# Sparse-attention stage: order of weight loads and bias rows, compressed bias by TensorE, gate row read from DRAM, gate products with stationary weights

## What is computed

```python
def nsa_mixer(h, rel_bias, w_in, ...):           # 16 heads of 64, 4 key/value groups
    q, kc, vc, ks, vs, kw, vw, gl = jnp.split(h @ w_in, cuts, axis=-1)
    kc = rms_norm(compress_blocks(kc, ...)); vc = compress_blocks(vc, ...)   # 31 compressed keys
    gates = jax.nn.sigmoid(gl).reshape(b, t, G, R, 3)
    dist_c = tq[:, None] - cmp_end[None, :]       # cmp_end = 16 n + 31
    lg = einsum(q, kc) * scale + bias_tbl[:, :, t5_bucket(dist_c)]
    p_c = masked_softmax(lg, dist_c >= 0);  o_c = einsum(p_c, vc)
    # o_s: the same with selected keys ks, vs; o_w: with the window's keys kw, vw; both with
    # bias_tbl[..., t5_bucket(distance)] over all distances
    o = gate[..., 0:1] * o_c + gate[..., 1:2] * o_s + gate[..., 2:3] * o_w
    return o @ w_out
# around it: mod = silu(c) @ ada_w + ada_b; shift, scale, gate = split(mod)
#            x = x + gate * nsa_mixer(rms_norm(x) * (1 + scale) + shift, ...)
```

## Time and profile before

| | us |
|---|---|
| three runs, median (lowest to highest) | 3502.08 (3494.92 to 3509.1) |
| the profiled execution, its own time | 3497.12 |
| its span in the trace | 3495.3 |
| PE busy in the span | 3260.8 (93%) |
| DVE, ACT, POOL busy | 2040.7, 1438.8, 155.5 |

### The profile page before, as it was taken

The page is one execution under the profiler, slowest core; times in us unless marked ns, Lnnn a source line. Parts: engine busy times, 40 slices in busy tenths (PEclk is TensorE's granted clock), DMA queues, the critical chain, the costliest instruction groups (busy, mean ns, idle before and its releaser), DMA issues. The chain is left out here.

```text
span 3495.3 us, 40219 instructions
## 1 busy us (share of the span) xinstructions
PE 3260.8 (93%) x15458; PEld 2605.5 (75%) x15458; DVE 2040.7 (58%) x2660; ACT 1438.8 (41%) x1946; POOL 155.5 (4%) x191
## 2 busy tenths in 40 slices
PE   7999998999999999998999969788999879999995
PEld 6888776788878888757888858545688658877884
DVE  4554426545545553354554445354788768868886
ACT  4222225322232222353222132264588646646884
POOL 0000000000000000000000000242000000001000
PEclk9999999999999999999999989799999989999998
DMA  5332230333223321341332141300799731119995
GB/s 200 127 144 108 101 108 3 151 138 144 108 91 145 144 109 53 139 115 79 138 156 114 60 150 37 73 1 25 299 419 416 286 120 61 61 52 396 417 415 211
DMA packets 96872, 534.19 MB, mean 153 GB/s; under 512 B 18816, under 2 KB 19712, under 8 KB 48336
## 3 DMA queue, kind: packets, MB, share of 16 engines
q1 hardware_dynamic: 85488, 491.24, 36.8%
q0 software_dynamic: 6624, 24.12, 1.8%
q10 hardware_dynamic: 4608, 16.78, 1.2%
HBM read 508.95 MB, written 32.06 MB: 155 GB/s over the span
## 5 line engine op out<-in xcount | busy, mean ns | idle before, releaser
L453 ACT ACTIVATE ffn_silu_gate<-ffn_gate_up 128x512 f32<-128x512 f32 x88 | 52.6, 598 | 960.3 <-PE ffn_gate_up L117 960.3
L515 DVE TENSOR_TENSOR ffn_product<-ffn_silu_gate,ffn_gate_up 128x512 f32<-128x512 f32 x88 | 60.5, 688 | 558.5 <-ACT ffn_silu_gate L453 558.5
L2620 DVE TENSOR_TENSOR moe_low<-moe_raw,moe_high 128x2048 fp32r<-128x2048 f32 x144 | 326.5, 2286 | 30.8 <-ACT moe_high L2537 30.7
L115 PE MATMUL ffn_down<-ffn_down_high,ffn_hid_high 128*128 128x512 f32 x704 | 282.6, 401 | 1.5 <-DVE x_tok L539 1.3
L539 DVE SCALAR_TENSOR_TENSOR x_tok<-ffn_down,x_tok 128x512 f32<-128x512 f32 x352 | 232.8, 687 | 82.6 <-PE ffn_down L117 81.2
L116 PE MATMUL ffn_down<-ffn_down_low,ffn_hid_high 128*128 128x512 f32 x704 | 281.0, 399 | 0.0
L117 PE MATMUL ffn_down<-ffn_down_high,ffn_hid_low 128*128 128x512 f32 x704 | 280.4, 398 | 0.0
L115 PE MATMUL ffn_gate_up<-ffn_h_high,w 128*128 128x512 f32 x704 | 280.2, 398 | 0.0
L116 PE MATMUL ffn_gate_up<-ffn_h_low,w 128*128 128x512 f32 x704 | 278.4, 395 | 0.0
L2537 ACT ACTIVATE moe_high<-moe_raw 128x2048 fp32r<-128x2048 f32 x144 | 274.2, 1917 | 9.9 <-PE moe_bank L117 9.9
L117 PE MATMUL ffn_gate_up<-ffn_h_high,w 128*128 128x512 f32 x704 | 278.2, 395 | 0.0
(11 more groups left out here) (609 smaller groups left out, 7174.0 us busy)
## 6 DMA issues: line engine op xcount, KB each, us to landing
moe_raw<-in_moe_w SPq DMA_DIRECT2D x192, 1024.0 KB, 8.3
ffn_raw_gate_up<-in_ffn_gate_up SPq DMA_DIRECT2D x85, 1024.0 KB, 6.3
ffn_ada_w<-in_ada_w SPq DMA_DIRECT2D x32, 1536.0 KB, 7.1
ffn_raw_down<-in_ffn_down SPq DMA_DIRECT2D x88, 512.0 KB, 3.4
mixer_w_raw<-in_mix_w SPq DMA_DIRECT2D x22, 1024.0 KB, 5.2
hgrn_w_raw<-in_hgrn_w SPq DMA_DIRECT2D x19, 1024.0 KB, 5.2
moe_y<-moe_y ACTq DMA_DIRECT2D x32, 512.0 KB, 9.4
nsa_w_raw<-in_nsa_w SPq DMA_DIRECT2D x13, 1024.0 KB, 5.6
```

The lines of the kernel that those rows point to most:

```text
L115: pe.matmul(out, lhsT[0], rhs[0], start=first, stop=False)
L453: act.activation(silu_gate[slot][:, :], gate_up_ps[2 * slot][:, :], ACT.Silu).then_inc(silu_done, 1)
L515: dve.tensor_tensor(product[slot][:, :], silu_gate[slot][:, :], gate_up_ps[2 * slot + 1][:, :], ALU.mult)\
L2620: dve.tensor_tensor(low[n % SPLITS][:, :, :], raw[n % RAWS][:, :, :], high[n % SPLITS][:, :, :].bitcast(FP32), ALU.subtract)\
```

## The change

Four things. SyncE issues halves 3 and 4 before it waits for the bias rows, and half 5 before `bias_copies`. The compressed bias comes from PE: 31 products whose stationary operand is a slice of 128 distances of a reversed one-hot table (`buckets` is doubled to 1280 columns, its second half reversed) and whose moving operand is `table`, 16 columns, into `cmp_rows` (128 x 31 x 16); VectorE fills `cmp_bias` from that, and its wait for the strip moves to just before the selected attention. The gate row is read from DRAM with one broadcasting DMA issued after the strip; the rows are stored by three DMAs at the end of SyncE's work in the first mixer stage, and `diag` and the GROW products go. The gate products have the 48 gate weights stationary and 512 tokens moving, 24 in place of 96; the result is feature-major, takes its sigmoid so, and four transposes (GATES_T) bring it back.

```diff
 # mixer, block.sync
             weights.fill(sp, 4)
+            if layer == 0:
+                store_modulation(sp, chip, 0)
...
 # nsa, block.sync
             sp.dma_start(qT_flat[:, 0:2048], dram["nsa_cmp_w1"]).then_inc(w1_loaded, 16)
+            weights.fill(sp, 3, 5)
             banks.wait_for(sp, ROWS)
             banks.wait_for(sp, ROWS + 1)
             sp.dma_start(dram["bias_rows"], rows).then_inc(rows_stored, 16)
+            weights.fill(sp, 5, 6)
             sp.wait_ge(rows_stored, 16)
...
-            weights.fill(sp, 3, 10)
+            weights.fill(sp, 6, 10)
...
             sp.dma_start(strip[:, :, :], askew).then_inc(strip_loaded, 16)
+            sp.wait_ge(chip.mod_rows_stored[0], 48)
+            sp.dma_start(gate_row[:, :], dram["mod_rows"][0, 2].unsqueeze(0).broadcast_to([P, DM])).then_inc(gate_loaded, 16)
             store_modulation(sp, chip, 3)
 # nsa, block.tensor
-            pe.wait_ge(diag_ready, 1)
             for a in range(2):
-                bank = banks.open(pe, GROW[a])
-                for k in range(4):
-                    last = pe.matmul(bank[:, k * P:(k + 1) * P], chip.ones[:, :], diag[:, 4 * a + k, :],
+                bank = banks.open(pe, CBIAS[a])
+                for n in range(16 * a, min(16 * a + 16, NCMP)):
+                    at = 640 + 481 - 16 * n
+                    last = pe.matmul(bank[:, NH * (n % 16):NH * (n % 16) + NH], buckets[:, at:at + P], table[:, :],
                                      start=True, stop=True)
...
-            for t in range(TT):
-                at = slice(t * P, (t + 1) * P)
-                for k in range(KT):
-                    last = split_matmul(pe, bank[:, 48 * t:48 * t + 48], (norm.high[:, k, at], norm.low[:, k, at]),
-                                        (wg_high[:, k, :], wg_low[:, k, :]), k == 0, k == KT - 1)
+            for k in range(KT):
+                last = split_matmul(pe, bank[0:3 * NH, :], (wg_high[:, k, :], wg_low[:, k, :]),
+                                    (norm.high[:, k, :], norm.low[:, k, :]), k == 0, k == KT - 1)
...
+            banks.wait_for(pe, GATES)
+            bank = banks.open(pe, GATES_T)
+            for t in range(TT):
+                last = pe.transpose(bank[:, 48 * t:48 * t + 48], gatesT[:, t * P:(t + 1) * P], chip.ident[0:3 * NH, 0:3 * NH])
+            last.then_inc(banks.computed, 1)
-            for o in range(KTR - 4, KTR + 4):
+            for o in range(KTR - 4, OUT):
                 banks.wait_for(pe, o)
 # nsa, block.vector
-            dve.tensor_tensor(diag, chip.ident[:, :].unsqueeze(1).broadcast_to([P, KT, P]),
-                              chip.mod[:, 0, 2, :].unsqueeze(2).broadcast_to([P, KT, P]), ALU.mult).then_inc(diag_ready, 1)
...
-            dve.wait_ge(strip_loaded, 16)
             dve.wait_ge(bias_filled, 1)
-            strip_halves = strip[:, :, :].rearrange("p (a b r) c -> p a b r c", a=2, b=2)
+            row_halves = cmp_rows[:, :, :].rearrange("p n (a b r) -> p a b r n", a=2, b=2)
...
-                                        strip_halves[:, :, half, :, c:c + 16 * (NB[i] - 1) + 1:16]))
+                                        row_halves[:, :, half, :, 24 - 8 * i:24 - 8 * i + NB[i]]))
...
+            dve.wait_ge(strip_loaded, 16)
             fused_scores(0)
...
+            dve.wait_ge(gate_loaded, 16)
             modulated_residual(dve, chip, banks, OUT, gate_row, ex[3].rearrange("p a k -> p (a k)")[:, 0:512], own, x_added,
```

More of the change, by code:

```diff
@@ L1204, in nsa @@
         banks = Banks(s)
-        C, ROWS, Q, PEB, GROW, HID, CMP, CMPV = 0, 4, (6, 15), 10, (11, 13), (12, 14), 19, 20
-        K, CMPT, QT, V, GATES, KTR, OUT = 21, 25, 26, 34, 38, 39, 43
+        C, ROWS, Q, PEB, CBIAS, HID, CMP, CMPV = 0, 4, (6, 15), 10, (11, 13), (12, 14), 19, 20
+        K, CMPT, QT, V, GATES, KTR, GATES_T, OUT = 21, 25, 26, 34, 38, 39, 43, 44
         half_rows = [P, KT, SEQ]
@@ L1228, in nsa @@
         k_squares = c_region[:, 0:512].rearrange("p (g d) -> p g d", d=HD)
-        diag = qT_flat[:, 3072:4096].rearrange("p (k n) -> p k n", k=KT)
-        buckets, rows = kT_flat[0:64, 0:640], kT_flat[0:NH, 640:1280]
+        buckets, rows = kT_flat[0:64, 0:1280], kT_flat[0:NH, 1280:1920]
         v = s.sb("v", [P, TT, 2, NG, HD])
@@ L1245, in nsa @@
         gate_row = s.sb("gate_row", [P, DM])
+        cmp_rows = s.sb("cmp_rows", [P, NCMP, NH])
         cmp_bias = k_region[:, 0:TT * NH * NCMP].rearrange("p (i h n) -> p i h n", h=NH, i=TT)
@@ L1250, in nsa @@
         ex = [k_region[:, 0:1024], k_region[:, 1024:2048], ex2[:, :], s.sb("exps3", [P, 1024])[:, :]]
+        gatesT = ex[3][0:3 * NH, 0:SEQ]
         ex = [e.rearrange("p (a k) -> p a k", a=2) for e in ex]
@@ L1262, in nsa @@
         q_normed, k_normed, kc_normed = s.sem("q_normed"), s.sem("k_normed"), s.sem("kc_normed")
-        diag_ready, bias_filled = s.sem("diag_ready"), s.sem("bias_filled")
+        gate_loaded, bias_filled = s.sem("gate_loaded"), s.sem("bias_filled")
         c_scores, c_read, c_max, c_shifted = s.sem("c_scores"), s.sem("c_read"), s.sem("c_max"), s.sem("c_shifted")
@@ L1274, in nsa @@
                    ROWS + 1: [piece(rows[:, 512:640], cols=(0, 128), rows=(0, NH))],
-                   GATES: [piece(gates[:, :, :].rearrange("p t c -> p (t c)"), cols=(0, 192), func=ACT.Sigmoid)],
+                   GATES: [piece(gatesT, rows=(0, 3 * NH), func=ACT.Sigmoid)],
+                   GATES_T: [piece(gates[:, :, :].rearrange("p t c -> p (t c)"), cols=(0, 192))],
                    PEB: [piece(peb[:, :], cols=(0, 2), rows=(0, 64))],
@@ L1295, in nsa @@
             outputs[HID[a]] = [piece(hid[:, a, :], cols=(0, NG * NCMP), rows=(0, 64), func=ACT.Silu, bias=peb[:, a:a + 1])]
-            outputs[GROW[a]] = [piece(gate_row[:, 512 * a:512 * a + 512])]
+            n = slice(16 * a, min(16 * a + 16, NCMP))
+            outputs[CBIAS[a]] = [piece(cmp_rows[:, n, :].rearrange("p n h -> p (n h)"), cols=(0, NH * (n.stop - n.start)))]
         def head(m, half):
@@ L1647, in _ @@
             evacuate(banks, dve, 1, outputs, V, OUT)
-            dve.wait_ge(strip_loaded, 16)
             dve.wait_ge(bias_filled, 1)
-            strip_halves = strip[:, :, :].rearrange("p (a b r) c -> p a b r c", a=2, b=2)
+            row_halves = cmp_rows[:, :, :].rearrange("p n (a b r) -> p a b r n", a=2, b=2)
             for i in range(TT):
-                c = 384 - P * i + 31
                 for half in range(2):
                     own(dve.tensor_copy(cmp_bias[:, i, 8 * half:8 * half + 8, 0:NB[i]].rearrange("p (a r) n -> p a r n", a=2),
-                                        strip_halves[:, :, half, :, c:c + 16 * (NB[i] - 1) + 1:16]))
+                                        row_halves[:, :, half, :, 24 - 8 * i:24 - 8 * i + NB[i]]))
             for i in range(TT):
@@ L2975, in constants @@
     f = np.float32
-    return {"moe_const": moe.astype(f), "hgrn_masks": masks, "hgrn_keep": keep, "nsa_buckets": distance_buckets(), "mix_near": near.astype(f), "mix_dft": dft.astype(f), "chan_dft": chan.astype(f), "alibi": alibi.astype(f)}
+    return {"moe_const": moe.astype(f), "hgrn_masks": masks, "hgrn_keep": keep, "nsa_buckets": np.concatenate([distance_buckets(), distance_buckets()[:, ::-1]], 1), "mix_near": near.astype(f), "mix_dft": dft.astype(f), "chan_dft": chan.astype(f), "alibi": alibi.astype(f)}
 def distance_buckets():
```

## The result

The changed kernel took **3462.94 us** (median of four runs, 3460.43 to 3470.81) against 3503.83 (3494.92 to 3509.10, four runs) before it on the same chip: a ratio of 0.989 [0.9863, 0.9916], so 1.1% less time. The forecast was 3465, between 3452 and 3480. The profiled execution took 3462.03 us, 35.1 less than the one before; its span is 3460.0.

A forecast was written before the change was run, and what follows sets the result against it. One chain bounded by PE, apart from two waits in the attention stage. Terms -19.1 - 1.6 + 7.3 - 11.4 - 1.5 - 10.4 = -36.7 us take the profiled 3497.1 to 3460.4, or 3465 on the median's scale; range 3452 to 3480.

The forecast's parts named there:

- two holes: PE waits in the attention stage: 19.07 us for weights in the second projection, 17.34 us before the compressed transposes.
- front hole: PE's wait inside the second projection, blamed on weights queued behind bias_copies: 19.07 us go, plus 1.6 from the clock.
- rival A: The second projection's wait stays because something other than the queue holds half 3; 3486 us, 4%.
- The bias products: 31 new 16-column products on PE, part low clock and part high: +7.3 us net, ends +2.7 and +10.3.
- Rival E: All 62 bias instructions cost only their 128 stationary columns at the high clock, 6.8 us; 3462 us, 10%.
- one-column products: Narrow PE products ahead of the bias products: taken at 4 us, the clock falling at their end.
- compressed scores: PE's score products after the key transposes: held at 11.43 us, with +-2 us for the clock.
- sure to half a microsecond: The gate products: 24 of 512 columns taking 5.5 us in place of 16.95, a gain of 11.4 us.
- The strip: Its wait, moved before the fused scores: landing after 20.4 us hidden by 1.1 us; second bias addition 10.4 us earlier.
- rival B: The strip becomes the limit, landing at 30 us with DMAs queued behind it; 8.5 us come back, 3474 us, 8%.
- C: Cheap TensorE: bias products overlap as the compressed scores do (+2.7 us) and scores stay fast; 3459 us, 10%.
- D: Slower than before: PE never regains the high clock through three projections (+66 us) and gates; 3536 us, 2%.

The follow-up runs named there:

- u1: The changed kernel with weight halves 3 to 9 again all behind the 5 MB bias-row copy; 3484.87 us, 0.9964 of the kernel before.
- u3: The changed kernel with the old gate products, 96 of 48 moving columns and no transposes back; 3480.1 us, 0.9951 of the kernel before.
- a3: The kernel before with only the 16-column bias products, gate row from DRAM and moved strip wait; 3501.24 us, ratio 1.001.
- after_again: The changed kernel, unedited, profiled a second time; 3469.03 us against 3506.69 for the kernel before.
- u2: The changed kernel with the compressed bias copied from the strip after the old wait, bias products made but unused; 3470.99 us, 0.9915 of the kernel before.
- b1: The changed kernel with each bias product issued between two compression products instead of in two blocks; 3476.81 us, 0.9935 of the kernel before.
- a2: The kernel before with only the gate products changed, weights stationary and four transposes back; 3489.61 us, ratio 0.9972.
- b2: The changed kernel with bias products between compression products and one-column products spread over the second projection's second half; 3474.87 us, 0.9927 of the kernel before.
- b3: The changed kernel with the first sixteen bias products moved ahead of the second projection; 3463.88 us, 0.9892 of the kernel before.

## Why the prediction was right, point by point

**The reading of the two holes held.** The front hole went whole (-20.9, forecast -19.1 - 1.6), and u1 brought it back by the queue's order alone. So rival A is refuted. Half 5, half 6 and the bucket table cost nothing, as expected. The other warning, that the element-wise stores could lengthen the first mixer by 20 to 60 us, did not come: the stage began 1.35 us later.

**The bias products cost what was chosen between the bounds**, +7.7 for +7.3, and in this profile for the stated reason: 32 instructions at the low clock (6.94 us, 0.217 each), 30 at the high one (3.45 us, 0.115 each). Rival E would have had 6.8 us for all; 10.4 were measured, and in the second profile 11.9. The split in two halves is less firm than it looks. Six profiles issue these products in the same order: the first one, u3 and a3 have the forecast's 6.9 and 3.5 us, but after_again has 6.36 and 5.57, u1 6.32 and 5.51, u2 5.64 and 4.21. So it is in part luck that the first profile has one block wholly low and the other wholly high; over all six the term is +7.2 to +9.3.

**Two terms were missing or off, and they cancel.** The one-column products took 1.4 us more in this profile, in which the clock fell inside them; in a3, where it did so too, they took 5.17 us for the 5.24 here, and 3.82 in after_again, u1, u2 and u3, where it held to their end. The prediction left them at their old cost. It also held the compressed scores at 11.43 us; they took 9.95, at the full clock for their first 4 us (10.96 in the second profile). The prediction named that case ("if the scores ran wholly at the high clock, that little is had") without putting it in the sum. The sum of -36.7 agreeing with -36.73 is thus partly luck: the terms that the clock sets are good to 1 or 2 us, and the stage before itself to 2.

**The gate products** came out to a tenth: 5.51 us, and 2.89 us to the scores for the 3.0 forecast. What they replaced is less firm, 14.99 to 17.86 us in the five profiles that have it, so "sure to half a microsecond" was said of the new products and does not hold for the difference. What the prediction did not price is what this part does for the scores behind it: about 1.5 us by the means of the two groups of profiles given with u3.

**The strip** was the margin to look at, 1.1 us by the forecast and 3.5 in the trace. The step that was mis-sized is its landing, 20.4 us carried over from the earlier trace rows; it took 16.1. The 20.4 goes with the modulation's stores right behind it in the queue (20.0 to 20.5 us in three profiles), and the change put the gate row between (13.8 to 18.7 in nine). The chain was mis-sized too: it reached the fused scores 19.7 us after the strip's issue, since the scores were quicker, so a strip that took 20.4 us would have held them up by 0.7. The two errors again work against each other. (The chain's last piece, 7.1 us, does not follow from its stated working, 8.4 less a quarter of 3.96, which is 7.4; the trace has 7.06.) The prediction had seen this hand ("something behind it may hold its completion") but expected it to work against the change (rival B). In u2 the strip landed in 18.7 us; against the 19.7 of the changed kernel's chain a margin of 1.0 would have been left.

**Rivals C and D.** C's sum, 3459, is within the scatter of the measured time, but its ground isn't there: the bias products took 0.115 and 0.217 us an instruction at the two clocks, not the 0.049 and 0.094 of the compressed scores, and that the scores overlap was the author's reading, which no run shows. D did not come: the clock was at 0.98 by 2095.5 and, after it had fallen once more, at 1.00 from 2106, and the next projection to gates took 72.51 us as before. b1 shows it was no idle worry: 35 us at the low clock, from a small change in the order, though the projection behind it lost only 1.1 us.

**What gave the time.** Weights ahead of the bias copies 21 to 24 us, gate products 10 to 12 alone and 15 in company. The bias part takes 10 to 12 us off the back and puts 9 on the front; alone it is worth nothing (1.001), beside the new gate products about 3 us in the stage (u1 against a2), which the times do not resolve. The median fell 40.9 us where the profiled executions differ by 35.1; the interval (29 to 48 us) holds both.

## What to carry to other kernels

In a shared DMA queue, put the loads that the bounding engine waits for ahead of bulk copies that are needed later; here that was worth 21 to 24 of the stage's 36.7 us and cost no work. Keep the wide dimension moving and the narrow one stationary: here it took the gate products from 16.95 to 5.51 us, and the 16 key transposes behind them from 3.67 to 1.91 us. Before a wait is bought off with work on the bounding engine, price that work at the lower clock if it is a run of narrow products (here 0.217 us an instruction for 0.115): in each of the thirteen profiles the clock fell to 0.50 in or right behind such runs.

## What the runs showed of the hardware beyond what was expected

- Compression products (64 stationary columns, 124 moving) in a row took 6.9 us for 32 instructions at either clock: 18 fall in 3.5 us at 0.50 (2092 to 2095.5 in the changed kernel) and 16 in 3 us at 1.00 (2096 to 2099). Products of 16 columns nearly doubled their time from 1.00 to 0.50 (0.115 to 0.217 us).
- Where these two kinds alternate, a set of four took 1.13 us at the low clock (b1) and 0.87 at the high one (b2); its parts in rows of one kind take 0.87 and 0.66 in the changed kernel. By that a change of kind costs an estimated 0.13 and 0.10 us. The clock stayed at 0.50 for 35 us in b1, though in the changed kernel it came back within a row of compression products (0.98 in the window from 2095.5). What in the switch costs the time is not shown.
- The low clock lasted past the narrow products that it fell in: with these ahead of the projection, it was 0.50 for the first 5.1 us of the dense projection behind them, which lost 2.4 us (24.4 for 22.0, b3).
- A 4 MB load landed 5.5 to 6.0 us later with 4 KB element-wise stores directly behind it in the queue (20.0 to 20.5 us, three profiles) than with a weight load there (14.5, one profile).
